# The first pair's query expansion and rotation moved ahead of the last two projection tiles

## What is computed

```python
proj = h @ lp['w_in']
q = (rmsnorm(q_a, lp['q_norm_g']) @ lp['w_q_b']).reshape(B, L, MLA_HEADS, QK_NOPE + QK_ROPE) * SOFTMAX_SCALE
...
kn, vv = kv_expand(c_kv, lp['w_kv_b'])
...
q_pe_rot = axial_rope(q_pe, row, col)
...
vc = v.reshape(B, L // GMLP_CHUNK, GMLP_CHUNK, GMLP_GROUPS, GMLP_W // GMLP_GROUPS)
sv = jnp.einsum('gpq,bnqgc->bnpgc', lp['gmlp_ws'], vc) + lp['gmlp_bs'].T[:, :, None]
branch_c = (u * sv.reshape(B, L, GMLP_W)) @ lp['w_gmlp_out']
...
pooled = jnp.stack([centred_mean_minus_self(g, w) for g, w in zip(groups, POOL_WINDOWS)], axis=2)
```

## Time and profile before

| | |
|---|---|
| median of 3 runs | 2649.79 us (2649.6 to 2650.01) |
| profiled execution, its own time | 2648.95 us |
| span of its trace | 2647.1 us, 44389 instructions |
| PE busy | 2404.7 us, 91% of the span |
| PE weight loads | 2228.2 us, 84% |
| DVE busy | 1807.2 us, 68% |
| ACT busy | 555.8 us, 21% |
| POOL busy | 1332.7 us, 50% |
| mean granted clock of PE | 0.951 of full speed |

### The profile page before, as it was taken

One profiled execution on the slowest core, in us unless ns is written; L12 is line 12 of the kernel. 1 busy time (PEld: TensorE's weight loads), 2 busy tenths in 40 slices (PEclk: granted clock), 3 DMA queues, 4 the chain that ended last, 5 costly groups with the idle time before them and its releaser, 6 DMA issues.

```text
span 2647.1 us, 44389 instructions
## 1 busy us (share of the span) xinstructions
PE 2404.7 (91%) x14854; PEld 2228.2 (84%) x14854; DVE 1807.2 (68%) x2357; ACT 555.8 (21%) x989; POOL 1332.7 (50%) x1240
## 2 busy tenths in 40 slices
PE   5897989999997999999959888899999799999996
PEld 5894548999986999999959744699999689999986
DVE  5558765554489898976573786555436888989566
ACT  1203442111121111123211144410111211111232
POOL 2458314555553656565435761065555445656551
PEclk9998999999997999999969989899999799999997
DMA  5210002333321323322212101033332223323221
GB/s 195 80 55 13 26 24 96 97 113 121 121 90 32 117 87 123 91 72 68 64 45 75 34 11 40 31 125 96 116 121 92 70 80 100 115 84 100 71 64 52
DMA packets 100491, 212.04 MB, mean 80 GB/s; under 512 B 10208, under 2 KB 17824, under 8 KB 100384
## 3 DMA queue, kind: packets, MB, share of 16 engines
q1 hardware_dynamic: 84832, 151.66, 19.6%
q10 hardware_dynamic: 15552, 59.02, 6.2%
HBM read 207.71 MB, written 2.93 MB: 80 GB/s over the span
## 4 chain that ended last, share of the span: by engine, by line
PE 55%; DVE 17%; DVEq 16%; issue 6%; ACT 5%; POOLq 1%; DMA 1%; ACTq 0%; POOL 0%; SPq 0%
PE ps L539 31%; PE ps L883 9%; DVEq L1795 4%; PE ps L559 4%; DVEq L1382 3%; PE ps L755 3%; DVE ada_part L1379 3%; DVEq L1801 3%; DVE up_y L1793 2%; PE ps L701 2%; DVE x L1403 1%; PE ps L572 1%; ACT up_x L1234 1%; DVE yb L1401 1%; PE ps L744 1%
## 5 line engine op out<-in xcount | busy, mean ns | idle before, releaser
L470 POOL TENSOR_SCALAR w_hi<-w_raw 128x512 fp32r<-128x512 f32 x552 | 378.7, 686 | 1107.9 <-PE ps L539 237.5
L472 POOL TENSOR_TENSOR w_lo<-w_raw,w_hi 128x512 fp32r<-128x512 f32 x552 | 769.8, 1395 | 81.4 <-issue 1.4
L539 PE MATMUL ps<-h_hi,w_hi 128*128 128x322 f32 x2688 | 627.5, 315 | 5.3 <-POOL w_lo L472 5.3
L539 PE MATMUL ps<-h_lo,w_hi 128*128 128x322 f32 x2688 | 623.6, 313 | 0.0
L539 PE MATMUL ps<-h_hi,w_lo 128*128 128x322 f32 x2688 | 620.3, 312 | 0.0
L539 PEld LDWEIGHTS ps<-h_hi,w_hi 128*128 128x128 f32 x2688 | 455.5, 191 | 8.7 <-POOL w_lo L472 7.4
L539 PEld LDWEIGHTS ps<-h_lo,w_hi 128*128 128x128 f32 x2688 | 458.2, 191 | 0.0
L539 PEld LDWEIGHTS ps<-h_hi,w_lo 128*128 128x128 f32 x2688 | 458.2, 191 | 0.0
L1379 DVE SCALAR_TENSOR_TENSOR ada_part<-ada_raw,cond,ada_part 128x384 f32<-128x384 f32 x448 | 342.2, 805 | 17.1
L1798 DVE SCALAR_TENSOR_TENSOR up_y<-up_x,par,up_y 128x644 f32<-128x644 f32 x176 | 216.0, 1267 | 13.9 <-issue 12.7
L1815 DVE TENSOR_TENSOR a_lo<-act,a_hi 128x644 fp32r<-128x644 f32 x84 | 130.0, 1549 | 116.1 <-ACT a_hi L1255 113.7
(11 more groups left out here) (254 smaller groups left out, 3577.6 us busy)
## 6 DMA issues: line engine op xcount, KB each, us to landing
w_raw<-in_w_lin_dram SPq DMA_DIRECT2D x360, 256.0 KB, 2.6
ada_raw<-in_w_ada_dram ACTq DMA_DIRECT2D x32, 1536.0 KB, 6.6
w_raw<-in_w_merge_dram SPq DMA_DIRECT2D x144, 256.0 KB, 2.7
ada_pre<-in_w_ada_dram ACTq DMA_DIRECT2D x4, 2048.0 KB, 14.6
w_raw<-in_w_merge_dram SPq DMA_DIRECT2D x48, 128.0 KB, 2.0
pw<-in_w_pair_dram SPq DMA_DIRECT2D x8, 640.0 KB, 3.9
x<-in_x_dram SPq DMA_DIRECT2D x8, 322.0 KB, 7.7
out_y_dram<-x SPq DMA_DIRECT2D x8, 322.0 KB, 2.3
```

The lines of the kernel that those rows point to most:

```text
L470: pool.tensor_scalar(w_hi[:, s, 0:n * P], raw, 1.0, 0.0, ALU.mult, ALU.add)
L472: pool.tensor_tensor(w_lo[:, s, 0:n * P], raw, w_hi[:, s, 0:n * P], ALU.subtract).then_inc(w_split[s], 1)
L539: last = pe.matmul(ps[:, 2 * s + j, 0:HALF], w, a[:, j * HALF:(j + 1) * HALF], start=(k == 0 and i == 0), stop=(k == total - 1 and i == 2))
```

## The change

On PE, the expansion of the first pair's two query heads comes ahead of tiles 14 and 15, and the waits for `qkv_ready` and `ctx_loaded` move with it. On ACT, the copies of these heads come between the copy of tile 13 and that of tile 14; the output DMAs stay behind tile 15. On DVE, `expand` is split into `rotate_queries` and `expand_keys`; for the first pair the rotations stand ahead of `gated_input(1)`, with a drain in front, and the key copy stays where it was. Nothing is added or left out in what is computed.

```diff
@@ PE
                     last.then_inc(set_full[c], 1)
-                p1_tile(14)
-                p1_tile(15)
-                assert tuple(uses) == (6, 6, 6, 6), uses
-
-
                 pe.wait_ge(qkv_ready, L + 1)
                 pe.wait_ge(ctx_loaded, (L + 1) * 48)
...
                 for hd in range(2):
                     expand_q(0, hd, first_use, 0)
+                p1_tile(14)
+                p1_tile(15)
+                assert tuple(uses) == (6, 6, 6, 6), uses
+
                 expand_k(first_use, 1)
                 expand_v(first_use, 1)
@@ ACT
+                for c in range(2):
+
+                    s = tile_done(10 + 3 * c)
+                    ac.activation(two(br[:, 2 + c, :]), halves(s), ACT.Tanh, scale=0.5).then_inc(set_empty[s], 1)
+                    if c == 1:
+                        for hd in range(2):
+                            expanded_q(0, hd, first_use, 0)
+                    s = tile_done(11 + 3 * c)
+                    ac.activation(two(br[:, 4 + c, :]), halves(s), ACT.Copy).then_inc(set_empty[s], 1)
+                    copied(s)
...
-                for hd in range(2):
-                    expanded_q(0, hd, first_use, 0)
...
                 expanded_kv(0, first_use, 1)
@@ DVE
                 pool(0)
+                def rotate_queries(p):
+                    n = L * N_PAIRS + p
+                    for hd in range(2):
+                        dv.wait_ge(q_part, n * 2 + (hd + 1))
+                        sample = slice(SAMPLE0, SAMPLE0 + DEC_SEQ)
+                        rotate(q_rot[64:96, hd, :], q_raw[64:96, hd, sample], q_raw[96:P, hd, sample])
+                        dv.drain()
+                        dv.sem_inc(q_ready, 1)
+
+                def expand_keys(p, use, k):
+                    n = L * N_PAIRS + p
+                    dv.wait_ge(set_full[0], use(0, k + 1) + 1)
+                    dv.tensor_copy(k_t[0:QK_NOPE, 1, :], line(0, NKEY, 64, P)).then_inc(k2_ready, 1)
+                    dv.wait_ge(k2_ready, n + 1)
+                    dv.wait_ge(k_ready, n + 1)
+                    dv.sem_inc(set_empty[0], 1)
...
                     for c0, m, g in REGIONS:
                         dv.tensor_tensor(br[:, 6 + c, c0:c0 + m], br[:, 6 + c, c0:c0 + m], hx[:, c, c0:c0 + m], ALU.mult)
+                dv.drain()
+                rotate_queries(0)
                 gated_input(1)
...
                 def expand(p, use, k):
...
+                    rotate_queries(p)
+                    expand_keys(p, use, k)
...
-                expand(0, lambda s, k: set_use(L, "expand", s, k), 0)
+                expand_keys(0, lambda s, k: set_use(L, "expand", s, k), 0)
```

More of the change, by code:

```diff
@@ L1041, in _ @@
                     ac.activation(two(br[:, 6 + c, :]), halves(s), ACT.Gelu).then_inc(set_empty[s], 1)
[L1042 to L1063, removed]
                 def expanded_q(p, hd, use, k):
@@ L1123, in first_use @@
                     return set_use(L, "expand", s, k)
-                for hd in range(2):
-                    expanded_q(0, hd, first_use, 0)
+                for c in range(2):
[7 more added lines that the diff above has]
+                    copied(s)
+                    s = tile_done(12 + 3 * c)
+                    ac.wait_ge(pool_x_free, L * 3 + (c + 1))
+                    p0, in_first = 2 * EDGE + SEQ, HALF - SAMPLE0
+                    ac.activation(pool_x[:, EDGE:EDGE + SEQ], ps[:, 2 * s, 0:SEQ], ACT.Copy)
+                    ac.activation(pool_x[:, p0:p0 + in_first], ps[:, 2 * s, SAMPLE0:HALF], ACT.Copy)
+                    ac.activation(pool_x[:, p0 + in_first:p0 + DEC_SEQ], ps[:, 2 * s + 1, 0:DEC_SEQ - in_first], ACT.Copy)\
+                        .then_inc(set_empty[s], 1)
+                    copied(s)
+                assert uses == [4, 4, 6, 6], uses
+                ac.wait_ge(qkv_ready, L + 1)
+                ac.dma_start(ckv_out[bass.ds(L, 1)].rearrange("a p c n -> (a p) c n"), ckv[:, :, KEYS:NKEY]).then_inc(qkv_out, 16)
+                ac.dma_start(kpe_out[bass.ds(L, 1)].rearrange("a p n -> (a p) n"), k_t[QK_NOPE:QK, 0, KEYS:NKEY]).then_inc(qkv_out, 16)
                 expanded_kv(0, first_use, 1)
```

## The result

The changed kernel takes 2653.77 us (median; 2651.45 to 2655.69), the kernel before, timed beside it, 2649.60 us (2644.47 to 2652.12). The ratio is 1.0019, 95% interval 1.0012 to 1.0026: about 4 us slower. The sign was forecast, the size was not: the forecast was 2660.5, and 2653.77 lies just under its range. The profiled execution took 2653.77 us around a span of 2652.0 (before: 2648.95 around 2647.1).

What follows compares the result with a forecast made beforehand. PE held 55% of the chain, DVE with its queue 33%. Scores 5.9 us later (14.6 - 9.27 + 0.6), less 0.5 credit, give 5.4 a layer, 10.8 in all: 2660.5 us, range 2654 to 2666.

Steps and rivals of the forecast that it cites:

- Step 1: PE, ahead of the query expansion, waits for DVE to empty PSUM sets 0 and 1: 6.2 us lost.
- Steps 2 and 3: Query expansion ahead of tiles 14 and 15 delays them 6.5 us; half clock behind the stall costs 1.9 us more.
- Rivals 1 and 4: Clock costs the tiles nothing, 2656.7 us, chance 0.15 (1); PE does not wait, 2644.2 us, chance 0.04 (4).
- Rival 2: Clock comes back late behind PE's stall: 4.3 us instead of 1.9, 2665.4 us in all; chance 0.18.
- Step 4: Both query rotations on DVE leave the chain, -9.27 us a layer, hidden with 3.9 us to spare before the pooling pass.
- Step 5: PE's second pooling product, now right ahead of the scores, starts at half clock: 2.3 us; scores 5.9 us late.
- rival 3: DVE's second pooling pass gets cheaper beside POOL's convolution, up to 6.2 us a layer, total about 2648; chance 0.08.
- Step 6: Credit at the first two scores, which run less at half clock: 0.5 us taken, range nothing to 1.9.
- exp table load: On ACT, ends near 239.1, first exp due about 240.2; a slip of over 1.1 us would reach the chain.

Runs made afterwards that it cites:

- 14: The changed kernel, unchanged, timed and profiled a second time: 2654.02 us, ratio 1.0020.
- experiment 3: Changed kernel with DVE emptying the gating product's sets 0 and 1 ahead of its first pooling pass: 2651.34 us, ratio 1.0011.
- Experiment 2: Changed kernel with six idle matmuls on PE ahead of the query expansion and six ahead of the second pooling product: 2650.99 us, ratio 1.0004.
- 9: Kernel before with eleven matmuls nobody reads on PE, in the idle time ahead of the first scores: 2651.10 us, ratio 1.0004.
- 13: Repeat, with more rounds, of the kernel before with eleven idle matmuls ahead of the first scores: 2650.69 us, ratio 0.9999.
- 6: Changed kernel with POOL's convolution of chunk 0 held until DVE's second pooling pass is done: 2650.88 us, ratio 1.0009.
- 10: Kernel before with POOL's convolution held until the first pair has been through, timed: 2629.45 us, ratio 0.9926.
- 7: Changed kernel with POOL's convolution held until the first pair has been through, a single execution: 2643.26 us.
- 11: Changed kernel with POOL's convolution held until the first pair has been through, timed: 2646.54 us, ratio 0.9990.
- experiment 1: Kernel before with nine matmuls nobody reads on PE, in the idle time ahead of the first scores: 2648.31 us, ratio 0.9999.

## Why the prediction was right in sign and wrong in size

**Step 1, the stall: right.** 5.95 us measured (5.94 in 14), 6.2 forecast, with the releaser that was named; experiment 3 takes it away by moving the release alone.

**Steps 2 and 3, expansion and clock: right.** 8.80 and 9.03 us against 6.5 + 1.9 = 8.4. Experiment 2 puts 2.0 and 2.3 us of it down to the clock. Tile 15 ends 14.55 us later in the first layer, 14.6 forecast. Rivals 1 and 4 fall with this. Rival 2, a price of 4.3 us here, falls too.

**Step 4, the rotations: right.** Hidden, with 3.40 and 3.58 us to spare where 3.9 were forecast; put back, they cost 9.8 us a layer.

**Step 5, the pooling product: right.** From its start to the first scores it is 2.30 us in the first layer and 2.30 to 2.31 in the other three, 2.3 forecast (2.51 to the end of its last matmul, which overlaps the scores, as the step says). Yet the scores are 4.5 and 4.8 us late, 5.0 on the mean of four layers, where 5.9 were forecast. What differs is a silent assumption of the steps before: that the second pooling pass keeps its length. From its start to the pooling product it took 12.23 us before, 10.85 after (11.1 and 12.2 in 14). This is rival 3's mechanism in part: the pass is slowed by POOL wherever it lies, by an amount that depends on how the two engines' instructions meet. I had it as all or nothing. On the mean of four layers it is worth 0.9 us a layer; the 2.7 from which it would have decided were not reached.

**Step 6, the credit: the term that was mis-sized.** I took 0.5 us, with 1.9 as the most, since I counted two scores and then expected DVE to set the pace. Measured, from first scores to weighted product, it is 2.5 us in both layers of the first execution, -0.3 and +1.5 in the other: 1.55 on the mean. The step's argument holds in the chain: only the first two scores gain, then DVE paces, although all of PE's work in the old order is at half clock for the first 8 us. But these two scores gained 1.8 and 1.7 us where the clock was back early, near the end of the range that I had given, and 0.5 and 0.7 where it was back late: 1.2 on the mean. The last transposes ahead of the weighted product, which the step put at nothing, gave 0.6 in every layer. DVE's part took 0.2 off, all of it from the one layer in which it met POOL's work badly. Experiments 9 and 13, which change nothing but the clock, gain 2.6 to 3.2 us, 2.2 of them on the two scores.

**The sum.** On the mean of four layers the weighted product is 3.4 us late, 5.4 forecast: 1.1 of the difference is the credit, 0.9 the pooling pass. The other 1.1 us goes between the first and the last weighted product, which take 148.8 us after (148.0 to 150.2) and 150.0 before (148.5, 151.4). The prediction had nothing there; the layers of one kernel differ by more than this, so it may be chance, and no run shows that the change makes it. 3.4 - 1.1 = 2.3 a layer, 4.6 in all. So about a third each of the 3.1 us that are missing a layer is the credit, the pooling pass and this stretch; that they all fell to the same side is in part luck. PE's line of the weighted products shows the end of it (count, duration ns min/median/max, first and last start us), first before, then after:

```profile
L755 PE MATMUL ps<-probs_t,v_pair x160: 592/592/1117, 254.8 to 1698.7; 128*64 128x512 f32 x160
```

```profile
L750 PE MATMUL ps<-probs_t,v_pair x160: 592/592/1117, 257.4 to 1703.3; 128*64 128x512 f32 x160
```

The last one starts 4.6 us later, and the span is 4.9 longer: behind the second layer's pairs little more is won or lost. Of the 4.6 us, 0.6 lie ahead of the first layer's gating product (190.30 against 189.68), which the change does not touch.

**What stays open.** Why the pairs behind the first take between 148 and 153 us from one layer to the next. In 9 and 13 they took 148.0 to 153.3 us (151.6 on the mean), 1.6 more than before, and so gave back over half of what the clock had won; the totals show no gain at all. That the gain of the first head reaches the end in the changed kernel, and not there, is therefore seen in the sums but not explained. The exp table load, which I named as late next, ends 0.3 us ahead of the first exp and did not reach the chain:

```profile
237.04 1.28 ACT L1065 ACT_TABLE_LOAD   x1
238.62 0.79 ACT L1065 ACTIVATE probs<-ps,small 128x640 f32<-128x640 f32 x1 [0.29 <-DVE small L1649]
```

## What to carry to other kernels

Work moved ahead in a queue takes the waits of its new place with it: look for what frees the buffers it writes, and price the stall, the cold clock behind it, and the clock that later work then gets. For the last, follow the chain: only instructions that stand in it gain. When each reordering of one engine gives the same time, the stage is set by another; here DVE beside POOL's convolution set most of it, and one wait that put the convolution later gave about 20 us, where the reordering lost 4. And a term that hangs on how two engines' instructions meet differs between layers of one execution; take it from several of them, and as a range.

## What the runs showed of the hardware

DVE's additions of two SBUF tiles in the pooling pass took 0.85 us with no convolution on POOL beside them (experiments 6 and 10) and 1.29 to 2.23 us beside it in the kernel before; the two rotations took 4.67 us against 9.27. The whole pooling pass took twice its time (6.26 and 12.65). The Trainium skill, "SBUF — State Buffer", section "Summary: rules for kernel authors", has the rule that of a DVE instruction with two SBUF inputs and a GpSimd one that reads SBUF the second to issue waits for the first. The runs agree, though in the changed kernel one addition in the same pass was spared (0.85, then 2.06).

The granted clock did not come back after a fixed time. In the expansion, behind 5.95 us of idle time, it was at half clock for 4.2 and 4.7 us (3.3 and 4.7 in experiment 14); behind 3.75 us of idle time, in experiments 6, 7 and 11, for 3.0 to 6.2 us, so the shorter stall did not cost less clock. Behind the first scores it was at half clock for 8.6 and 8.8 us before the change, for 1.0 and 1.2 us in one execution of the changed kernel and for 3.7 and 3.2 us in another. It also fell again within the head: over the whole way to the weighted product its mean was 0.64 before and 0.78 to 0.90 after.

With 1.92 us of idle time ahead of the first scores (experiment 1) the clock was lost 1.2 us after PE had started again; with 0.20 us (experiments 9 and 13) it was lost only after 8.7 to 9.3 us of scores and transposes with waits between them. The 1.84 us of idle time ahead of the gating product, with dense matmuls before and behind it, did not lose it: the two tiles behind ran in 14.50 us.
